# Tile-wise openings of a fourth weight unit, and compressed scores with the keys stationary, in a decoder trunk of six sublayers

## What is computed

```
h = x
for i in range(2):                       # layer 0 mixes with NSA, layer 1 with FoX
    h = h + 0.5 * rms_norm(swiglu(rms_norm(h, g0), w_gate, w_up, w_down), g1)
    h = h +       rms_norm(mixer(rms_norm(h, g2)), g3)
    h = h + 0.5 * rms_norm(swiglu(rms_norm(h, g4), w_gate, w_up, w_down), g5)
```

## Time and profile before

| | |
|---|---|
| median of 3 runs | 1038.15 us (1036.49 to 1038.55) |
| the profiled execution | 1037.07 us, its span 1035.3 us |
| PE busy / DVE busy / ACT busy | 1018.8 / 641.4 / 518.5 us |
| granted clock of TensorE | 0.999 |

### The profile page before, as it was taken

The page is one execution under the profiler, slowest core; times in us unless marked ns, Lnnn a source line. Parts: engine busy times, 40 slices in busy tenths (PEclk is TensorE's granted clock), DMA queues, the critical chain, the costliest instruction groups (busy, mean ns, idle before and its releaser), DMA issues.

```text
span 1035.3 us, 14391 instructions
## 1 busy us (share of the span) xinstructions
PE 1018.8 (98%) x5991; PEld 871.9 (84%) x5991; DVE 641.4 (62%) x772; ACT 518.5 (50%) x710; POOL 109.4 (11%) x210
## 2 busy tenths in 40 slices
PE   8999999999999999999999999999999999999997
PEld 7888888898756898888889888888988689888886
DVE  5656555755696755656576655556648776555554
ACT  5554544544564554454454454445546554444542
POOL 1000000312252200000030000001103320000000
PEclk9999999999999999999999999999999999999999
DMA  8767766578203265655556655655674336656552
GB/s 255 254 202 258 235 219 199 170 222 261 102 2 122 82 220 188 203 180 187 203 163 204 204 179 188 203 183 183 204 249 170 111 103 204 188 181 201 193 176 79
DMA packets 138377, 189.58 MB, mean 183 GB/s; under 512 B 7395, under 2 KB 120392, under 8 KB 138313
## 3 DMA queue, kind: packets, MB, share of 16 engines
q1 hardware_dynamic: 133734, 172.83, 51.8%
q0 software_dynamic: 4432, 15.77, 4.6%
q10 hardware_dynamic: 146, 0.07, 0.0%
HBM read 185.99 MB, written 1.09 MB: 181 GB/s over the span
## 4 chain that ended last, share of the span: by engine, by line
PE 91%; DVE 4%; POOL 2%; issue 1%; ACT 1%; DMA 0%; DVEq 0%; POOLq 0%; ACTq 0%
PE ps L1154 88%; PE ps L1522 1%; DVE normed L808 1%; ACT work L540 1%; DVE probT_buf L930 1%; PE ps L1342 1%; POOL ms L411 1%; POOL rstd L413 1%; DVE res L792 1%; DVE wlo L766 1%; POOL ms_half L407 0%; DVE normed L904 0%; DVE normed L784 0%; DMA gain_row<-in_norm_g 0%; ACT work L630 0%
## 5 line engine op out<-in xcount | busy, mean ns | idle before, releaser
L758 DVE TENSOR_TENSOR wlo<-raw,whi 128x2048 fp32r<-128x2048 f32 x150 | 344.2, 2295 | 143.7 <-ACT whi L514 143.7
L1154 PE MATMUL ps<-xhl,whi 128*128 128x512 f32 (+1 forms) x1600 | 387.6, 384 | 0.0
L1154 PEld LDWEIGHTS ps<-xhl,whi 128*128 128x128 f32 x1600 | 283.0, 189 | 51.5 <-issue 2.4
L514 ACT ACTIVATE whi<-raw 128x2048 fp32r<-128x2048 f32 x150 | 286.1, 1907 | 22.7 <-DMA raw<-in_fox_w_in 9.2
L1154 PEld LDWEIGHTS ps<-xhl,wlo 128*128 128x128 f32 x1600 | 215.7, 190 | 16.2 <-DVE wlo L766 1.7
L1154 PE MATMUL ps<-xhl,wlo 128*128 128x256 f32 (+1 forms) x1600 | 221.0, 282 | 0.9 <-DVE wlo L766 0.9
L1154 PE MATMUL ps<-whi,xhl 128*128 128x256 f32 (+1 forms) x640 | 132.7, 318 | 0.9 <-DVE xhl L816 0.9
L1154 PE MATMUL ps<-whi,hhi 128*128 128x512 f32 x320 | 124.9, 390 | 0.0
L1154 PE MATMUL ps<-wlo,hhi 128*128 128x512 f32 x320 | 124.9, 390 | 0.0
L1154 PE MATMUL ps<-whi,hlo 128*128 128x512 f32 x320 | 124.5, 389 | 0.0
L1154 PEld LDWEIGHTS ps<-whi,xhl 128*128 128x128 f32 x640 | 101.4, 190 | 10.3 <-issue 3.2
(11 more groups left out here) (170 smaller groups left out, 760.1 us busy)
## 6 DMA issues: line engine op xcount, KB each, us to landing
raw<-in_ffn_w_down SPq DMA_DIRECT2D x44, 1024.0 KB, 4.9
raw<-in_ffn_w_gate SPq DMA_DIRECT2D x40, 1024.0 KB, 5.3
raw<-in_ffn_w_up SPq DMA_DIRECT2D x40, 1024.0 KB, 5.4
raw<-in_fox_w_in SPq DMA_DIRECT2D x10, 1024.0 KB, 5.5
raw<-in_nsa_w_in SPq DMA_DIRECT2D x8, 1024.0 KB, 5.4
raw<-in_nsa_w_out SPq DMA_DIRECT2D x4, 1024.0 KB, 5.2
raw<-in_fox_w_out SPq DMA_DIRECT2D x4, 1024.0 KB, 4.8
g_post<-in_norm_g POOLq DMA_DIRECT2D x6, 512.0 KB, 4.0
```

The lines of the kernel that those rows point to most:

```text
L514: nc.scalar.activation(whi[:, u % RING, :], raw_of(u), ACT.Copy).then_inc(w_hi, 1)
L758: nc.vector.tensor_tensor(wlo[:, u % RING, :], raw_of(u), whi[:, u % RING, :].bitcast(F32), ALU.subtract).then_inc(w_lo, 1)
L1154: return nc.tensor.matmul(out_, l, r, start=start, stop=stop)
```

## The change

Four openings (sublayers 1, 2, 3 and 5; FoX and sublayer 0 keep theirs) take in a fourth unit. `twin_tile` is replaced by `twin_high`, which multiplies only the high weights, one tile of tokens at a time, and `twin_low`, which multiplies the low weights with all 256 tokens at once. Unit u0+3 is opened with tile 0 right after u0+2, into the banks YB and YB+1, which are free by then; `product_T` and the NSA gates move to YB+2. So that u0+3 can be opened this early, ACT rounds it ahead of `split_x` of tile 1, and DVE does `split_x` of tile 1 ahead of the second half of the low part of u0+2.

The compressed scores have the keys stationary now (two rows of 16 columns for each head pair, 32 in all) and the queries move: 4 matmuls with 256 columns. The result has keys on the partitions, so ACT copies it out (`scores_out`) and PE transposes it back with two transposes (`turn_scores`), in the middle of the projection of u0+8 for r = 0 and at the end of stage 4 for r = 1. The DVE and ACT steps on the logits of r = 1 stand one stage later.

```diff
         def up_bank(f, c):
+            return YB if f and c == 1 else GB
...
             if kind == "nsa":
-                return (GB, UB)[k] if k < 2 else GB + 2 * (1 - k % 2)
+                return (GB, UB, OB, YB)[k] if k < 4 else GB + 2 * (1 - k % 2)
...
+                    def scores_out(r):
+                        act.wait_ge(sc_keys, r + 1)
+                        if r:
+                            act.wait_ge(sc_mm, 1)
+                        nc.scalar.activation(scoresT, ps[:, MB if r else YB + 2, 0:S], ACT.Copy).then_inc(sc_copied, 1)
...
                     if kind == "nsa":
+                        scores_out(0)
                         evacuate(8)
...
                     for b in range(2):
                         square(s + 1, 0, 1, b)
+                    if KINDS[s + 1] != "fox":
+                        hi(u + 3)
                     split_x(s + 1, 1)
...
-                    lo_part(u + 2, 1)
-                    split_x(s + 1, 1)
+                    if KINDS[s + 1] == "fox":
+                        lo_part(u + 2, 1)
+                        split_x(s + 1, 1)
+                    else:
+                        split_x(s + 1, 1)
+                        lo_part(u + 2, 1)
...
+            def twin_high(u, bank, t, before={}):
+                wh = wcols(u % RING)[0]
+                tile = slice(t * P, (t + 1) * P)
+                n = 0
+                pe.wait_ge(w_hi, u + 1)
+                for a in range(2):
+                    o_ = ps[:, bank + a, :].rearrange("p (b n) -> p b n", b=2)[:, :, tile]
+                    for k in range(KT):
+                        if n in before:
+                            before[n]()
+                        n += 1
+                        mm(o_, wh[:, k, a * P:(a + 1) * P], xhl[:, k, :, tile], t == 0 and k == 0, False)
+
+            def twin_low(u, bank):
+                pe.wait_ge(w_lo, u + 1)
+                wl = wcols(u % RING)[1]
+                for a in range(2):
+                    for k in range(KT):
+                        last = mm(ps[:, bank + a, 0:S], wl[:, k, a * P:(a + 1) * P], xhi[:, k, :], False, k == KT - 1)
+                last.then_inc(unit_done, 1)
...
-                third(u0 + 2, OB, 0, {12: T1[0], 15: T1[1]})
+                high(u0 + 2, OB, 0, {12: T1[0], 15: T1[1]})
+                if feature:
+                    twin_high(u0 + 3, YB, 0)
                 tokens(u0, u0 % RING, GB, (1,), 4 * s + 2)
                 tokens(u0 + 1, (u0 + 1) % RING, UB, (1,))
-                third(u0 + 2, OB, 1, {16: product_T} if product_T else {})
+                high(u0 + 2, OB, 1)
+                if feature:
+                    if product_T:
+                        product_T()
+                    twin_low(u0 + 2, OB)
+                    twin_high(u0 + 3, YB, 1)
+                    twin_low(u0 + 3, YB)
...
                     def compressed_scores(r):
-                        for t in range(TT):
-                            for pair in range(4 * r, 4 * r + 4):
-                                c0 = 256 * r + (t * 8 + 2 * (pair - 4 * r)) * NC
-                                last = mm(ps[:, MB if r else YB + 2, c0:c0 + 2 * NC], qT[:, pair, t * P:(t + 1) * P], kcmp[:, 2 * pair // G, :, :], True, True)
-                        last.then_inc(sc_mm, 1)
+                        for pair in range(4 * r, 4 * r + 4):
+                            c0 = 32 * (pair - 4 * r)
+                            last = mm(ps[c0:c0 + 32, MB if r else YB + 2, 0:S], kcmp[:, 2 * pair // G, :, :].rearrange("p a c -> p (a c)"),
+                                      qT[:, pair, :], True, True)
+                        last.then_inc(sc_keys, 1)
+
+                    def turn_scores(r):
+                        pe.wait_ge(sc_copied, r + 1)
                         for t in range(TT):
+                            last = nc.tensor.transpose(ps[:, MB if r else YB + 2, S + t * P:S + (t + 1) * P], scoresT[:, t * P:(t + 1) * P], ident)
                         last.then_inc(sc_mm, 1)
```

More of the change, by code:

```diff
@@ L210, in trunk @@
         YB, GB, UB, OB, MB = 0, 4, 5, 6, 7
+        PTB, NGB = YB + 2, YB + 2
         CMB = [YB + 3, MB]
@@ L727, in _ @@
                     evacuate(nproj - 1)
-                    attend(kind, u0 + nproj + 2, {5: lambda: compressed_exp(1)} if kind == "nsa" else {})
+                    attend(kind, u0 + nproj + 2, {3: lambda: scores_out(1), 6: lambda: compressed_exp(1)} if kind == "nsa" else {})
                     for k in range(2, 3):
@@ L842, in hidden_lo @@
                 dve.wait_ge(hhi_ready, NCH * f + c + 1)
-                src = prod_sb if c else ps[:, YB, :]
+                src = prod_sb if c else ps[:, PTB, :]
                 hi_, lo_ = (xhi[:, 0:2, :], xlo[:, 0:2, :]) if c == NCH - 1 else (hhi[:, c % 2, :, :], hlo[:, c % 2, :, :])
@@ L1124, in _ @@
                         attend(kind, u0 + nproj + 2, {0: lambda: lo(u0 + 11), 1: first_compressed, 2: compressed_values, 3: first_transposed,
-                                                      4: lambda: compressed_logits(1), 5: lambda: compressed_max(1), 7: lambda: compressed_probs(1),
+                                                      5: lambda: compressed_logits(1), 6: lambda: compressed_max(1), 8: lambda: compressed_probs(1),
                                                       9: lambda: later_transposed(2), 10: lambda: later_transposed(3)})
@@ L1210, in twin_features @@
                 last.then_inc(unit_done, 1)
-            def twin_tile(u, bank, t, before={}):
-                wh, wl = wcols(u % RING)
+            def twin_high(u, bank, t, before={}):
+                wh = wcols(u % RING)[0]
                 tile = slice(t * P, (t + 1) * P)
                 n = 0
[L1217 to L1234, removed]
+                pe.wait_ge(w_hi, u + 1)
[13 more added lines that the diff above has]
+                last.then_inc(unit_done, 1)
             def tokens_tile(u, bank, t, before={}):
@@ L1371, in open_sublayer @@
                     return
-                third = tokens_tile if KINDS[s] == "fox" else twin_tile
+                feature = KINDS[s] != "fox"
+                high = twin_high if feature else tokens_tile
                 tokens(u0, u0 % RING, GB, (0,), 4 * s)
                 tokens_tile(u0 + 1, UB, 0)
-                third(u0 + 2, OB, 0, {12: T1[0], 15: T1[1]})
+                high(u0 + 2, OB, 0, {12: T1[0], 15: T1[1]})
+                if feature:
+                    twin_high(u0 + 3, YB, 0)
                 tokens(u0, u0 % RING, GB, (1,), 4 * s + 2)
                 tokens(u0 + 1, (u0 + 1) % RING, UB, (1,))
-                third(u0 + 2, OB, 1, {16: product_T} if product_T else {})
+                high(u0 + 2, OB, 1)
[5 more added lines that the diff above has]
+                    twin_low(u0 + 3, YB)
             def setup():
@@ L1628, in later_T @@
                         last.then_inc(probcT_mm, 1)
-                    for k in range(2, 9):
-                        if k >= 3:
-                            project(k)
-                        if k == 2:
-                            gates(YB, 0, 48)
+                    for k in range(3, 9):
+                        if k >= 4:
+                            project(k, (lambda: turn_scores(0)) if k == 8 else None)
+                        if k == 3:
+                            gates(NGB, 0, 48)
                         if k == 4:
```

41 lines of the change are left out of this document (22 added, 19 removed).

## The result

The changed kernel takes 1029.27 us (median of 6 runs, 1028.64 to 1029.62), the kernel before 1038.11 us on the same chip (median of 6). The ratio is 0.9915, with a 95% interval of 0.9902 to 0.9927: 8.8 us faster. The profiled execution took 1029.26 us, against 1037.07 before, and its span is 7.9 us shorter.

The account below looks back on a forecast made before the run. PE bounds the kernel, busy 98% of the span. Four openings (7.4 us) and two sets of scores (0.6 each) sum to 8.6 us: 1028.5 from the profiled 1037.07, 1029.5 by the median; forecast 1029.0, range 1026.5 to 1032.5.

Parts of the forecast that it names:

- The pace of PE: In the openings, matmuls of 128 columns cost about 0.115 us, nearly as much as 256 columns at about 0.12 us.
- columns set the price: Rival for the openings' low products: 128 columns cost half of 256, gain only 1.8 us, 1035.2 us; chance 0.05.
- a sign of being wrong: In an opening, the 16 matmuls of 256 columns at low weights take more than 0.12 us each.
- The front of an opening: PE goes on with u0+3 instead of waiting behind tile 0's high part: 0.16 of the 1.86 us per opening.
- What has to arrive earlier: ACT's rounding of u0+3 ahead of x: its DMA lands after 5.7 us, hidden with 0.3 us to spare, costed at nothing.
- ACT blocks before x: Rival in the openings: u0+3's DMA lands late, PE starves; slower, 1040 us if it takes 10.0 us; chance 0.05.
- The next wait: At u0+4 in three FFN openings PE needs DVE's addition, covered by 0.14 us: no wait, bound 0.3 us each.
- Late supply: Rival: PE waits for the additions at u0+4 or rounding of u0+5; gain 6.5 us, 1031 to 1032; chance 0.16.
- all DMAs of the ring from u0+7 on: Issued up to 1.9 us earlier, as PE is, with the same distance to their use.
- The scores, r = 0: Compressed scores go from 1.71 us to 1.08 with two transposes: gain 0.6 us, bounds 0.2 to 0.7.
- 8 x 0.113: Price of the new score matmuls at r = 0: 8 records at 0.113 us from the compression product, 0.90 us.
- r = 1: Compressed scores in stage 4: gain 0.6 us; worth nothing if DVE is the bound there, up to 0.9 with slack.

Follow-up runs that it names:

- e6: Changed kernel with ACT's rounding of u0+3 put back behind the high part of x for tile 1: 1043.52 us, ratio to before 1.0057.
- e9: Changed kernel with four extra key products at r = 0, written by turns into two groups of 32 partitions: 1.42 us for the 16 records.
- e1: Changed kernel with SP issuing the DMA of NSA's u0+7 only when the four small copies have landed: 1027.99 us, ratio to before 0.9902.
- e7: Changed kernel with SP issuing the DMA of NSA's u0+7 only when PE has done the gate products: 1028.05 us, ratio to before 0.9906.
- e5: Changed kernel with the NSA opening as before, only the FFN openings and scores new: 1029.66 us, ratio to before 0.9921.

## Why the prediction was right, point by point

**The forecast** of 1029.0 us, range 1026.5 to 1032.5, held: 1029.27. But it came out of a sum with one term missing and others too small, and that they cancelled to within 0.3 us is luck. Against the profiled execution the sum was 8.6, and 7.8 was measured.

**The pace of PE** was read rightly. The low products of 128 columns cost 0.115 us like those of 256, and taking them away gave the 1.9 us. The rival that columns set the price is out. The stretch from tile 1 of u0 to u0+4 took 370.61 - 356.74 = 13.87 us; before, 374.06 - 358.54 = 15.52. The gain of 1.65 stands against 1.70 forecast: the 16 low products behind `product_T` take 2.00 us, 0.08 more than the 1.92 of the next 16. That is 0.125 each, over the 0.12 that I had named as a sign of being wrong; it costs 0.08 us in each FFN opening and changes nothing else.

**The front of an opening** was sized too small, "0.16 comes from the front". It is 0.3, so 1.97 in all and not 1.86. I subtracted the idle time of 0.23 from the start of the wait's end, but that idle time counts from the modelled end of the matmul before. The last one started at 356.10, the pace is 0.12, so PE could have issued at 356.22: 0.47 us stood empty, not 0.23.

**What has to arrive earlier** on ACT: right that PE does not see it, wrong in the 0.3 us to spare. The rounding in sublayer 2 had to wait for its DMA, which landed 6.2 us after its issue where I had taken 5.7, and ended at 354.33, while the transposed x was there some 0.1 us before; the 1.2 us behind it covered that. The rival "ACT blocks before x" did not come about, and e6 shows the opposite order to be the costly one.

**The next wait**, at u0+4, with "a cover of only 0.14 us": right. The addition ends 0.23 us before PE's start, and no wait is shown. Late supply did not come about.

**The scores, r = 0**: forecast 0.6, bounds 0.2 to 0.7, measured 0.9: from the start of the scores to the attention loop's first scores it is 7.47 us before (254.90 to 262.37) and 6.59 after (255.14 to 261.73), 0.88 less. The term that was mis-sized is "8 x 0.113": it measured 8 x 0.071. The row that I took it from, the compression product, writes to the two halves of the output partitions by turns, so that it has an overlap of two in it (by the two-group price of e9, 0.106); the new scores have that of four. I had looked at how many columns move, not at where it writes. **r = 1**: forecast 0.6, measured 0.86, under the upper bound of 0.9. The waits for L930 of 0.56 and 1.25 us became 0.35 and 0.62, with one of 0.32 ahead: the gain was not eaten.

**The step that failed** is the sentence that all DMAs of the ring from u0+7 on are issued "up to 1.9 us earlier" and "have the same distance to their use", with nothing put down for it. In NSA u0+7's came 4.5 us earlier. The distance holds for the units and the waits of the engines on them; but a DMA that moves in time also moves against other DMAs. u0+7's moved while the four copies behind DVE's `join` of u0+2 did not, being tied to an earlier DMA (u0+4, which hardly moved). They had not met before and met now, and it cost the full gain of one opening, 1.86 us. e1, e7 and e5 show this from three sides. The miss was hidden in the total because 0.4 from the fronts, 0.4 to 0.5 from the scores and some 0.5 in stretches without an edit came on top, and the median of the runs before lies 1.0 us above the profiled time (1038.11 against 1037.07), while after the change the two agree.

**A better version** comes out of this: e1, one added wait on SP, 1027.99 us, against 1037.98 before and 1029.56 for the change on the same chip.

## What to carry to other kernels

When a step is moved, list the DMAs that its completion releases, and for each look at what else is on the DMA engines at the new time: small copies on which someone waits should be issued before a big load, here by 1.0 us or more, if need be by holding the load back. Read PE's pace from starts, and an empty stretch as the distance of two starts less the pace. Where a stationary operand is narrow, spread the products over column groups.

## What the runs showed of the hardware that I had not expected

Plain fp32 products with 32 stationary columns and 256 moving cost 0.213 us per record in one group of 32 output partitions, 0.106 in two groups by turns and 0.054 in four.

A 1 MB DMA issued amid four copies of 128 KB, 0.17 us behind the first and ahead of three, delayed the first from 2.5 to 4.4 us and the last three from 2.5 to 2.8 us to 6.3 to 6.6 us, and was itself late (8.1 us); issued 1.0 us behind the last of them it delayed nothing, and landed after 5.4 us.

Behind a wait of PE of 2.4 us in an opening the granted clock fell to 0.50 for some 2 us or more in two of four openings (e6), and in the two others, with the same wait, it did not.
